# Attention's first head: slabs rounded ahead of the stream's norm, evacuations ahead of the rope, swap ahead of the key pages

## The chip, the cores and the metric

One NeuronCore of a Trainium2 chip runs the whole program. The metric is the device time in microseconds (us) of one launch. Engines: TensorE (PE in the profile; PEld is its weight load), VectorE (DVE), ScalarE (ACT), GpSimd (POOL), and SyncE (SP), which issues all DMAs here.

## The reference

One inference step of a two-layer decoder, width 1024, on a prompt of 1024 tokens and 8 samples of 8 tokens, side by side as T = 1088 columns. Layer 0 is a gated delta rule and a squared-ReLU MLP. Layer 1 is differential attention over 8 heads, each with two maps of 64 channels, and a second MLP. What the change touches is where layer 1 begins:

```python
kv = rmsnorm(h, ln_kv) @ w_kv                       # shared keys and values
k = rope(rmsnorm(kv_k.reshape(..., 8, 2, 64), k_norm), pos)
q = rope(rmsnorm((rmsnorm(h, ln_mix) @ w_q).reshape(..., 8, 2, 64), q_norm), pos)
s = q @ keys.T * 64 ** -0.5                         # keys: cached pages (samples), own keys
p = softmax(where(mask, s, min)); a = p[0] - lam * p[1]
```

The rope turns the first 16 of each map's 64 channels. The samples' cached keys lie in pages that `page_table` names (16 pages of 128 tokens).

## The kernel before

Activations are kept channel-major: `XH` and `XL` hold the stream as a high and a low part (128 x 8 chunks x 1092 columns, in three groups of 364). A product runs over *slabs* of weights, 1024 x 128. A slab is loaded by SyncE into one of two buffers (`load_slab`, L176), scaled by the norm's gain on GpSimd (`scale_slab`, L183), rounded to its high half on ScalarE (`hi_slab`, L189), and its low half is the difference, on VectorE (`lo_slab`, L193). `slab_products` (L203) then does, for each of 8 chunks, three products (high x high, high x low, low x high) by three column groups: 72 matmuls. Slab n's load waits for slab n-2's low half; its rounding waits for slab n-2's products. Semaphores are counters; `Steps.at(i, k)` is the value after step k of round i.

The order of work on each engine is written out by hand. Every engine executes its list in order, so an instruction that waits holds all behind it.

The last part of layer 0's MLP makes the stream's final chunks: a product into PSUM banks 0 to 2 and then one into 3 to 5, each added to `ACC` on VectorE (L1636, `mlp0.free`, numbers 94 and 95 are the last two), then `x_hi` on ScalarE (L1610), `x_lo` on VectorE (L1643, `x_ready`), and the squares summed on GpSimd (L1664).

Then attention's head 0, outside the loop over heads. Its three slabs are k (number 0), q (1) and v (2), in banks 0 to 2, 3 to 5 and 0 to 2:

- TensorE (`att_first_head_tensor`): slab 0's products, the sum of squares over the stream (three matmuls with ones, L2009, `b_sum`), slab 1's products with three `kq_sum` matmuls (L1903) in front of chunks 3, 4 and 5 (they sum the squares of k by map), slab 2's with those of q. Then, in `body`, transposes of the cached keys (L2027), of the new keys (L2043, they need all nine evacuated units, `b_ev.at(0)`, and k's rope), of the values (L2056), and the samples' scores against the cached keys (L2064, they need q's rope).
- ScalarE (`att_scalar`): the stream's norm, three Ln and an Exp into `RSTD` (`b_rs`); slab 1's rounding; squares, Ln and Exp for k; slab 2's rounding; the same for q; the rounding of head 1's k slab, `att_slab(0, 1, 0)`.
- VectorE (`att_vector`): evacuates slab 0 (three `unit_out`, L2407, times `RSTD`), makes ten constants (`constants`, L2393 to L2402, they wait for the constants' DMAs, `b_in`), slab 1's low half, k's norm (`normed`, L2417), slab 2's low half, k's rope in three steps (L2434, L2436, L2439), then evacuates slab 1, and so on; v is evacuated behind q's rope.
- SyncE (`att_sync`): when all of the stream and its sums are made, it loads the tables of the rope and other constants over the MLP's buffers (L1821), the page table (L1822), reads the 16 page numbers into registers (`value_load`, L1825), and goes on with slab 2, 16 pages of cached keys (`key_pages`, L1834), head 1's k slab, the swap of k's rope halves (`swap`, four small DMAs, L1842 and L1843, behind `b_nm`), head 1's q slab, and q's swap.
- GpSimd (`att_gpsimd`) scales slabs 1, 2, head 1's k and q, in this order.

The loop body over heads interleaves head h's attention with head h+1's products by a written order. It isn't changed.

Of the kernel before, what the change touches and what calls it, by code (L numbers as in the profile page):

```python
# [117 lines left out]
def program(nc, x_prompt, x_sample, cache_k, cache_v, page_table, state_delta, state_conv,  # L118
# [1609 lines left out]
    b_in = nc.alloc_semaphore("att_constants_in")  # L1728
# [51 lines left out]
    def att_load(sp, j, a, s):  # L1780
        src = w_q_b[0] if s == 1 else w_kv
        off = a * P + (D if s == 2 else 0)
        load_slab(sp, att_slab(j, a, s), src[:, ds(j * 2 * P + off, P)].rearrange("(k p) c -> p k c", p=P))
# [19 lines left out]


    def att_sync(sp):
        mlp0.x_ready(sp, KC - 1)
        sp.wait_ge(b_sum.sem, b_sum.at(0))
        tables = rope_tables()
        mask = np.zeros((P, 4 * P + NS), np.float32)
        q, k = np.arange(P)[:, None], np.arange(P)[None, :]  # L1810
        for n, full in enumerate((np.eye(P), np.where(k > q, NEG, 0.0))):
            for part in range(2):
                rows = full[part * B_HD:(part + 1) * B_HD]
                mask[:, (2 * n + part) * P:(2 * n + part + 1) * P] = np.concatenate([rows, rows])
        q, k = (np.arange(P) % NS)[:, None], np.arange(NS)[None, :]
        mask[:, 4 * P:] = np.where((q // NQ == k // NQ) & (k % NQ <= q % NQ), 0.0, NEG)
        for dst, a, name in ((COS[:, :], tables[:, 0], "c_cos"), (SIN[:, :], tables[:, 1], "c_sin"),
                             (BO64[:, :], np.kron(np.eye(2), np.ones((B_HD, B_HD))), "c_map_ones"),
                             (STK[:, :], np.concatenate([np.eye(NS)] * 2), "c_stack"),
                             (MASKF[:, :], mask, "c_masks")):  # L1820
            sp.dma_start(dst, nc.inline_tensor(np.ascontiguousarray(a.astype(np.float32)), name).ap()).then_inc(b_in, 16)  # L1821
        sp.dma_start(PGT[:, :], page_table.rearrange("b n -> (b n)").rearrange("(a n) -> a n", a=1)).then_inc(b_in, 16)  # L1822
        sp.wait_ge(b_in, 16 * 6)

        pages = [ds(sp.value_load(PGT[0:1, n:n + 1], min_val=0, max_val=cache_k.shape[0] - 1), 1)  # L1825
                 for n in range(NB * NPG)]

        def key_pages(h, before=None):
            head = ds(h, 1)
            for n in range(NB * NPG):  # L1830
                src = cache_k[pages[n], :, head, :, :].rearrange("a t b m d -> (a t b) (m d)")
                if n == 0 and before is not None:
                    sp.wait_ge(b_pv.sem, b_pv.at(before, SAMPLE_AT + 1))
                sp.dma_start(CP[:, n, :], src).then_inc(b_kin, 16)  # L1834

        def swap(a, i):
            s = i[1]
            i = 2 * i[0] + s
            sp.wait_ge(b_nm.sem, b_nm.at(i))
            for m in range(2):  # L1840
                one, two = (slice(m * B_HD + c * ROT // 2, m * B_HD + (c + 1) * ROT // 2) for c in range(2))
                sp.dma_start(SWP[one, :], KS[a][s][two, 0:T]).then_inc(b_dx, 16)  # L1842
                sp.dma_start(SWP[two, :], KS[a][s][one, 0:T]).then_inc(b_dx, 16)  # L1843

        att_load(sp, 0, 0, 2)
        key_pages(0)
        att_load(sp, 0, 1, 0)
        swap(0, (0, 0))
        att_load(sp, 0, 1, 1)
        swap(0, (0, 1))  # L1850

        def body(j, a):
            h = 2 * j + a
            last = is_head(j, a, H - 1)
            if not last:
                att_load(sp, j, a + 1, 2)
            head, cols_h = ds(h, 1), ds(h * P, P)
            for n in range(NB * NPG):
                src = cache_v[pages[n], :, head, :].rearrange("a t b d -> (a t b) d")
                if n == 0:  # L1860
                    sp.wait_ge(b_pt.sem, b_pt.at(h))
                elif n == NB * NPG - 1:
                    sp.wait_ge(b_kc.sem, b_kc.at(h))
                sp.dma_start(CP[:, n, :], src).then_inc(b_vin, 16)
            sp.dma_start(k_prompt[0].rearrange("t h m d -> t (h m d)")[:, cols_h].rearrange("(u p) c -> p u c", p=P),
                         KTM[:, 0:NT, :]).then_inc(b_ko, 16)
            sp.dma_start(k_sample.rearrange("b q h m d -> (b q) (h m d)")[:, cols_h], KTM[0:NS, NT, :]).then_inc(b_ko, 16)
            sp.wait_ge(b_vc.sem, b_vc.at(h))
            sp.dma_start(v_prompt[0].rearrange("t h d -> t (h d)")[:, cols_h].rearrange("(u p) c -> p u c", p=P),
                         VT[:, 0:NT, :]).then_inc(b_vo, 16)  # L1870
            sp.dma_start(v_sample.rearrange("b q h d -> (b q) (h d)")[:, cols_h], VT[0:NS, NT, :]).then_inc(b_vo, 16)
            if last:
                return
            if is_head(j, a, H - 2):
                proj_b.load(sp, 0, 0)
            else:
                att_load(sp, j, a + 2, 0)
            swap(1 - a, (h + 1, 0))
            key_pages(h + 1, before=h)
            if is_head(j, a, H - 2):  # L1880
                proj_b.load(sp, 0, 1)
            else:
                att_load(sp, j, a + 2, 1)
            swap(1 - a, (h + 1, 1))

        over_heads(sp, body)
# [97 lines left out]
    def att_first_head_tensor(pe):  # L1984
        for s in range(3):
            n = att_slab(0, 0, s)
            pe.wait_ge(w_lo.sem, w_lo.at(n.n))
            if s == 2:
                pe.wait_ge(b_ev.sem, b_ev.at(0, 3))
            for k in range(KC):  # L1990
                if s == 0:
                    mlp0.x_ready(pe, k)
                if s > 0 and 3 <= k < 6:
                    if s == 1 and k == 3:
                        pe.wait_ge(b_ct.sem, b_ct.at(NBC - 1))
                        pe.wait_ge(b_rs.sem, b_rs.at(0, 3))
                    elif s == 2 and k == 3:
                        pe.wait_ge(b_ln.sem, b_ln.at(0, 3))
                    elif k == 5:
                        pe.wait_ge(b_ln.sem, b_ln.at(s - 1, 1))  # L2000
                    kq_sum(pe, 0, s - 1, k - 3, 6 + (k - 3) % 2)
                mm = slab_products(n, 3 * (s % 2), XH, XL, [k], KC)
            mm.then_inc(w_used.sem, 1)
            if s == 0:
                pe.wait_ge(mlp0.sums.sem, mlp0.sums.at(KC - 1))
                for c in range(3):
                    if c == 2:
                        pe.wait_ge(b_rs.sem, b_rs.at(0, 1))
                    nc.tensor.matmul(PS[:, 6 + c % 2, 0:WIDTH[c]], ONES[:, :], SQA[:, c * GRP:c * GRP + WIDTH[c]],  # L2009
                                     start=True, stop=True).then_inc(b_sum.sem, 1)  # L2010

    def att_tensor(pe):
        pe.wait_ge(mlp0.free.sem, mlp0.free.at(95))
        att_first_head_tensor(pe)

        def body(j, a):
# [204 lines left out]

    def att_scalar(act):
        exp_ln_set()
        for c in range(3):
            act.wait_ge(b_sum.sem, b_sum.at(0, c + 1))
            nc.scalar.activation(RSTD[:, c * GRP:c * GRP + WIDTH[c]], PS[:, 6 + c % 2, 0:WIDTH[c]], ACT.Ln,
                                 scale=1.0 / D, bias=EPS).then_inc(b_rs.sem, 1)
# [2 lines left out]
        act.wait_ge(b_rs.sem, b_rs.at(0))  # L2230
        mlp0.x_ready(act, KC - 1)

        hi_slab(act, att_slab(0, 0, 1))
        for s in range(2):
            for g in range(3):
                att_square(act, 0, 0, s, g)
                if g >= 1:
                    att_ln(act, 0, s, g - 1, 6 + (g - 1) % 2)
            att_ln(act, 0, s, 2, 6)
            att_rstd(act, 0, s)  # L2240
            hi_slab(act, att_slab(0, 0, 2) if s == 0 else att_slab(0, 1, 0))

        def body(j, a):
            h = 2 * j + a
# [145 lines left out]
    def att_vector(dve):  # L2390
# [47 lines left out]
                dve.wait_ge(b_rp.sem, b_rp.at(i, 2))  # L2438
                nc.vector.tensor_tensor(t, t, SWP[:, :], ALU.add).then_inc(b_rp.sem, 1)  # L2439

        dve.wait_ge(b_rs.sem, b_rs.at(0))
        for s in range(3):
            dve.wait_ge(w_used.sem, w_used.at(att_slab(0, 0, s).n))
            for g in range(3):
                unit_out(0, s, g, 3 * (s % 2) + g)
            if s == 0:
                constants()
                lo_slab(dve, att_slab(0, 0, 1))
            if s < 2:
                normed(0, 0, s)  # L2450
                lo_slab(dve, att_slab(0, 0, 2) if s == 0 else att_slab(0, 1, 0))
                for step in range(3):
                    rope(0, 0, s, step)

        def body(j, a):
            h = 2 * j + a
# [259 lines left out]
```

## Time and profile before

| | |
|---|---|
| median of 3 runs | 3540.38 us (3538.64 to 3541.57) |
| profiled execution, its time | 3543.65 us |
| its span in the trace | 3541.8 us |
| mean granted TensorE clock | 0.967 |
| TensorE (matmuls) busy | 3308.3 us, 93% |
| VectorE, ScalarE, GpSimd busy | 43%, 32%, 17% |
| mean DMA rate | 45 GB/s |

The page gives averages over the whole program. The stretch that the change touches is some 90 us long, from 1914 to 2003 us; it is read from the timelines of each engine, with a view of windows that shows the TensorE clock which the throttle granted (1.00 is 2.4 GHz, 0.50 is 1.2 GHz). An instruction's idle time stands in brackets, with what ended it.

### The profile page before, as it was taken

How to read it: one execution, taken by the hardware profiler on the slowest of the kernel's cores; microseconds unless marked ns; L12 is line 12 of the kernel's file. 1: busy time of each engine (PE TensorE's matmuls, PEld its weight loads, DVE VectorE, ACT ScalarE, POOL GpSimd, SP SyncE). 2: the span in 40 equal slices, each digit the busy share in tenths (PEclk: the TensorE clock that was granted, in tenths of full speed). 3: DMA queues.
4: the chain of work that ended last, by engine and by line, in shares of the span. 5: the costliest groups of instructions: out<-in, count | busy, mean ns of one | idle time of the engine just before them, and what ended most of it. 6: DMA issues, size and time to landing. Idle time of an engine off the chain costs nothing. (4 is left out here: it accounts for less than half of the span.)

```text
span 3541.8 us, 59935 instructions
## 1 busy us (share of the span) xinstructions
PE 3308.3 (93%) x23951; PEld 3163.5 (89%) x23951; DVE 1521.3 (43%) x2295; ACT 1131.9 (32%) x2096; POOL 613.5 (17%) x421
## 2 busy tenths in 40 slices
PE   5899888988879999999998899999989999999998
PEld 4888878887869999999998788888879999999998
DVE  2555555555537222232224455555557232232222
ACT  3443444344431311111113344444551211111111
POOL 0212221123202311111112100000001311111110
PEclk7999999999969999999999999999999999999999
DMA  2010110011001111111111222222211111111111
GB/s 90 22 32 26 32 33 26 26 32 38 20 26 42 42 45 46 42 48 48 42 45 39 70 59 59 59 62 66 61 38 42 42 47 44 48 43 48 42 45 66
DMA packets 255565, 157.90 MB, mean 45 GB/s; under 512 B 10016, under 2 KB 252082, under 8 KB 255282
## 3 DMA queue, kind: packets, MB, share of 16 engines
q1 hardware_dynamic: 255306, 154.08, 15.1%
q8 instruction: 208, 3.41, 0.4%
q14 instruction: 51, 0.42, 0.0%
HBM read 133.39 MB, written 18.42 MB: 43 GB/s over the span
## 5 line engine op out<-in xcount | busy, mean ns | idle before, releaser
L203 PE MATMUL ps<-x_hi,w_hi 128*128 128x364 f32 (+1 forms) x2304 | 544.9, 344 | 18.5 <-DVE w_lo L193 11.9
L203 PE MATMUL ps<-x_lo,w_hi 128*128 128x364 f32 (+1 forms) x2304 | 510.2, 330 | 0.0
L203 PE MATMUL ps<-x_hi,w_lo 128*128 128x364 f32 (+1 forms) x2304 | 507.9, 329 | 0.0
L193 DVE TENSOR_TENSOR w_lo<-w_raw,w_hi 128x1024 fp32r<-128x1024 f32 x200 | 287.2, 1436 | 469.2 <-ACT w_hi L189 469.1
L189 ACT ACTIVATE w_hi<-w_raw 128x1024 fp32r<-128x1024 f32 x200 | 211.7, 1058 | 809.1 <-PE ps L203 594.2
L183 POOL TENSOR_TENSOR w_raw<-w_raw,params 128x1024 f32<-128x1024 f32 x120 | 237.3, 1977 | 1251.5 <-DMA w_raw<-in_w_in_a 446.3
L203 PEld LDWEIGHTS ps<-x_hi,w_hi 128*128 128x128 f32 x2304 | 396.9, 190 | 46.8 <-DVE w_lo L193 13.6
L203 PEld LDWEIGHTS ps<-x_lo,w_hi 128*128 128x128 f32 x2304 | 401.3, 189 | 0.0
L203 PEld LDWEIGHTS ps<-x_hi,w_lo 128*128 128x128 f32 x2304 | 400.9, 189 | 0.0
L1636 DVE TENSOR_TENSOR acc<-ps,acc 128x1092 f32<-128x1092 f32 x128 | 165.6, 1294 | 435.3 <-PE ps L203 435.3
L203 PE MATMUL ps<-hidden_hi,w_hi 128*128 128x364 f32 (+1 forms) x1536 | 339.2, 329 | 0.0
L203 PE MATMUL ps<-hidden_hi,w_lo 128*128 128x364 f32 (+1 forms) x1536 | 338.4, 328 | 0.0
L203 PE MATMUL ps<-hidden_lo,w_hi 128*128 128x364 f32 (+1 forms) x1536 | 338.3, 328 | 0.0
L1656 POOL TENSOR_TENSOR hidden_lo<-tmp,hidden_hi 128x1092 fp32r<-128x1092 f32 x64 | 162.9, 2545 | 798.7 <-ACT hidden_hi L1605 798.7
L203 PEld LDWEIGHTS ps<-hidden_lo,w_hi 128*128 128x128 f32 x1536 | 266.4, 189 | 0.0
L203 PEld LDWEIGHTS ps<-hidden_hi,w_hi 128*128 128x128 f32 x1536 | 266.2, 188 | 0.0
L203 PEld LDWEIGHTS ps<-hidden_hi,w_lo 128*128 128x128 f32 x1536 | 266.1, 188 | 0.0
L1603 ACT ACTIVATE tmp<-tmp 128x1092 f32<-128x1092 f32 x64 | 71.5, 1118 | 416.6 <-DVE tmp L1625 416.6
L1625 DVE SCALAR_TENSOR_TENSOR tmp<-ps,rstd 128x1092 f32<-128x1092 f32 x64 | 82.9, 1296 | 243.7 <-PE ps L203 235.5
L1896 PE MATMUL ps<-x_hi,w_hi 128*128 128x364 f32 (+1 forms) x504 | 175.9, 349 | 4.1 <-DVE mix L2407 3.9
L1896 PE MATMUL ps<-x_hi,w_lo 128*128 128x364 f32 (+1 forms) x504 | 165.2, 328 | 0.0
L1896 PE MATMUL ps<-x_lo,w_hi 128*128 128x364 f32 (+1 forms) x504 | 165.0, 327 | 0.0
(365 smaller groups left out, 5153.7 us busy)
## 6 DMA issues: line engine op xcount, KB each, us to landing
w_raw<-in_w_up SPq DMA_DIRECT2D x64, 512.0 KB, 3.9
w_raw<-in_w_down SPq DMA_DIRECT2D x64, 512.0 KB, 3.4
w_raw<-in_w_in_a SPq DMA_DIRECT2D x32, 512.0 KB, 4.2
w_raw<-in_w_kv SPq DMA_DIRECT2D x16, 512.0 KB, 3.8
cache_pages<-in_cache_k SPq DMA_DIRECT2D x128, 64.0 KB, 1.9
cache_pages<-in_cache_v SPq DMA_DIRECT2D x128, 64.0 KB, 1.9
x_in<-in_x_prompt SPq DMA_DIRECT2D x8, 512.0 KB, 4.4
state_sample<-in_state_delta SPq DMA_DIRECT2D x8, 512.0 KB, 4.0
```

The source lines that it names most:

```text
L183: nc.gpsimd.tensor_tensor(RAW[s.slot][:, :, :], RAW[s.slot][:, :, :], gain(g).unsqueeze(2).to_broadcast([P, KC, P]), ALU.mult).then_inc(w_ ...
L189: nc.scalar.activation(WH[s.slot][:, :, :], RAW[s.slot][:, :, :], ACT.Copy).then_inc(w_hi.sem, 1)
L193: nc.vector.tensor_tensor(WL[s.slot][:, :, :], RAW[s.slot][:, :, :], WH[s.slot][:, :, :].bitcast(F32), ALU.subtract).then_inc(w_lo.sem, 1)
L203: mm = nc.tensor.matmul(PS[:, bank + g, 0:WIDTH[g]], wt, x[:, k, g * GRP:g * GRP + WIDTH[g]], start=(k == 0 and t == 0), stop=(k == chunks ...
L1603: nc.scalar.activation(t, t, ACT.Square).then_inc(self.hid.sem, 1)
L1625: nc.vector.scalar_tensor_tensor(grouped(TMP[up][:, :]), banks(3 * op), 0.0, grouped(RSTD[:, :]), ALU.max, ALU.mult).then_inc(self.free.se ...
L1636: nc.vector.tensor_tensor(grouped(ACC[:, m, :]), banks(3 * ((op + a) % 2)), grouped(ACC[:, m, :]), ALU.add).then_inc(self.free.sem, 1)
L1656: nc.gpsimd.tensor_tensor(HID[par][1][:, s, :], TMP[up][:, :], HID[par][0][:, s, :].bitcast(F32), ALU.subtract).then_inc(self.lo.sem, 1)
L1896: mm = nc.tensor.matmul(PS[:, bank, 0:WIDTH[g]], w[s.slot][:, k, :], x[:, k, g * GRP:g * GRP + WIDTH[g]], start=(k == 0 and t == 0), stop= ...
```

## The change

Nothing is computed otherwise. In the stretch at head 0:

- SyncE issues slab 2's load first, in front of its waits for the stream and the sums; k's swap is issued in front of the 16 key pages, and head 1's two slab loads then follow the pages back to back.
- TensorE starts slab 0 when evacuation 94 is done (banks 0 to 2), and waits for 95 in front of slab 1. The `kq_sum`s move from chunks 3 to 5 to chunks 4 to 6. The wait for the made constants moves from slab 1 to slab 2; slab 1 waits instead for the constants' DMAs (`b_in`), in front of its first `kq_sum`.
- ScalarE rounds slab 1 in front of the stream's norm, and slab 2 right behind it, in front of k's squares.
- VectorE makes slab 1's low half first, evacuates slab 0, makes slab 2's low half, the constants, k's norm; then it evacuates slab 1 in front of k's rope; then q's norm, the low half of head 1's k slab, the evacuation of slab 2 (v), and q's rope last.

```diff
@@ att_sync @@
+        att_load(sp, 0, 0, 2)
         mlp0.x_ready(sp, KC - 1)
         sp.wait_ge(b_sum.sem, b_sum.at(0))
...
-        att_load(sp, 0, 0, 2)
+        swap(0, (0, 0))
         key_pages(0)
         att_load(sp, 0, 1, 0)
-        swap(0, (0, 0))
         att_load(sp, 0, 1, 1)
         swap(0, (0, 1))
@@ att_first_head_tensor @@
             pe.wait_ge(w_lo.sem, w_lo.at(n.n))
+            if s == 1:
+                pe.wait_ge(mlp0.free.sem, mlp0.free.at(95))
             if s == 2:
                 pe.wait_ge(b_ev.sem, b_ev.at(0, 3))
...
-                if s > 0 and 3 <= k < 6:
-                    if s == 1 and k == 3:
+                if s > 0 and 4 <= k < 7:
+                    if s == 1 and k == 4:
+                        pe.wait_ge(b_in, 16 * 6)
+                        pe.wait_ge(b_rs.sem, b_rs.at(0, 3))
+                    elif s == 2 and k == 4:
                         pe.wait_ge(b_ct.sem, b_ct.at(NBC - 1))
-                        pe.wait_ge(b_rs.sem, b_rs.at(0, 3))
-                    elif s == 2 and k == 3:
                         pe.wait_ge(b_ln.sem, b_ln.at(0, 3))
-                    elif k == 5:
+                    elif k == 6:
                         pe.wait_ge(b_ln.sem, b_ln.at(s - 1, 1))
-                    kq_sum(pe, 0, s - 1, k - 3, 6 + (k - 3) % 2)
+                    kq_sum(pe, 0, s - 1, k - 4, 6 + k % 2)
@@ att_tensor @@
-        pe.wait_ge(mlp0.free.sem, mlp0.free.at(95))
+        pe.wait_ge(mlp0.free.sem, mlp0.free.at(94))
@@ att_scalar @@
         exp_ln_set()
+        hi_slab(act, att_slab(0, 0, 1))
         for c in range(3):
...
-        hi_slab(act, att_slab(0, 0, 1))
+        hi_slab(act, att_slab(0, 0, 2))
         for s in range(2):
...
-            hi_slab(act, att_slab(0, 0, 2) if s == 0 else att_slab(0, 1, 0))
+            if s == 1:
+                hi_slab(act, att_slab(0, 1, 0))
@@ att_vector @@
-        dve.wait_ge(b_rs.sem, b_rs.at(0))
-        for s in range(3):
+        def first_units(s):
             dve.wait_ge(w_used.sem, w_used.at(att_slab(0, 0, s).n))
             for g in range(3):
                 unit_out(0, s, g, 3 * (s % 2) + g)
-            if s == 0:
-                constants()
-                lo_slab(dve, att_slab(0, 0, 1))
-            if s < 2:
-                normed(0, 0, s)
-                lo_slab(dve, att_slab(0, 0, 2) if s == 0 else att_slab(0, 1, 0))
-                for step in range(3):
-                    rope(0, 0, s, step)
+        lo_slab(dve, att_slab(0, 0, 1))
+        dve.wait_ge(b_rs.sem, b_rs.at(0))
+        first_units(0)
+        lo_slab(dve, att_slab(0, 0, 2))
+        constants()
+        normed(0, 0, 0)
+        first_units(1)
+        for step in range(3):
+            rope(0, 0, 0, step)
+        normed(0, 0, 1)
+        lo_slab(dve, att_slab(0, 1, 0))
+        first_units(2)
+        for step in range(3):
+            rope(0, 0, 1, step)
```

## Rows read from the trace of the kernel before

**Rows 1.** The page: busy time of TensorE, its share, its instructions.

```profile
PE 3308.3 (93%) x23951; PEld 3163.5 (89%) x23951; DVE 1521.3 (43%) x2295; ACT 1131.9 (32%) x2096; POOL 613.5 (17%) x421
```

**Rows 2.** TensorE's timeline: start, duration, line, operation, in brackets idle before and releaser.

```profile
1918.28 0.77 PE L203 MATMUL ps<-x_hi,w_hi 128*128 128x364 f32 x3 [3.40 <-DVE acc L1636]
...
1931.86 2.21 PE L2009 MATMUL ps<-sq_sum,ones 128*128 128x364 f32 x6
1944.94 1.28 PE L203 MATMUL ps<-x_hi,w_hi 128*128 128x364 f32 x3 [10.87 <-DVE w_lo L193]
...
1954.04 0.77 PE L1903 MATMUL ps<-kq_squared,map_ones 128*128 128x364 f32 x2
...
1956.14 0.77 PE L1903 MATMUL ps<-kq_squared,map_ones 128*128 128x364 f32 x2
...
1971.20 1.55 PE L1903 MATMUL ps<-kq_squared,map_ones 128*128 128x364 f32 x2 [5.30 <-ACT kq_squared L2188]
...
1992.11 2.15 PE L2043 MATMUL ps<-ident,k_even 128*128 128x128 f32 x9 [9.09 <-DVE mix L2407]
...
1997.68 3.82 PE L2064 MATMUL ps<-cache_keys_t,q_by_batch 128*128 128x256 f32 x16
```

**Rows 3.** Windows: stretch, length, busy time by engine (instructions), TensorE clock, DMA.

```profile
1919.60:1922.90 3.30, 3.30 (x13) 3.30 (x12) 1.11 (x1) 2.23 (x2) 2.22 (x1) 0.50 0.00 0
...
1992.10:1997.70 5.60, 5.59 (x27) 5.52 (x28) 0.36 (x3) 3.62 (x8) 0.00 (x0) 0.50 0.06 17
```

**Rows 4.** VectorE's timeline, end of the MLP to head 0.

```profile
1913.26 1.29 DVE L1636 TENSOR_TENSOR acc<-ps,acc 128x1092 f32<-128x1092 f32 x1
...
1919.41 1.30 DVE L1643 TENSOR_TENSOR x_lo<-acc,x_hi 128x1092 fp32r<-128x1092 f32 x1 [1.18 <-ACT x_hi L1610]
...
1958.61 1.35 DVE L2417 SCALAR_TENSOR_TENSOR k_even<-k_even,params,kq_rstd 128x1092 f32<-128x1092 f32 x1 [13.73 <-ACT kq_rstd L2201]
...
1964.67 1.29 DVE L2434 TENSOR_TENSOR kq_swapped<-kq_swapped,rope_sin 128x1088 f32<-128x1088 f32 x1 [3.57 <-DMA kq_swapped<-k_even]
...
1987.76 2.87 DVE L2439 TENSOR_TENSOR q_even<-q_even,kq_swapped 128x1088 f32<-128x1088 f32 x1
1990.55 1.41 DVE L2407 TENSOR_TENSOR mix<-ps,rstd 128x364 f32<-128x364 f32 x3
```

**Rows 5.** SyncE, page numbers into registers: durations ns min/median/max, first and last start.

```profile
L1825 SPq TENSOR_LOAD <-page_numbers x16: 263/267/493, 1940.3 to 1948.8; - x16
```

**Rows 6.** SyncE's timeline: DMA issues.

```profile
1949.36 0.40 SPq L176 DMA_DIRECT2D w_raw<-in_w_kv  x1
1949.95 8.16 SPq L1834 DMA_DIRECT2D cache_pages<-in_cache_k  x16
1958.15 0.43 SPq L176 DMA_DIRECT2D w_raw<-in_w_kv  x1
1959.99 0.81 SPq L1842 DMA_DIRECT2D kq_swapped<-k_even  x1
...
1962.89 0.44 SPq L176 DMA_DIRECT2D w_raw<-in_w_q_b  x1
```

**Rows 7.** Slab tiles, 1880 to 2010: durations ns min/median/max, first and last start.

```profile
L189 ACT ACTIVATE w_hi<-w_raw x7: 1040/1059/1062, 1882.6 to 2007.4; 128x1024 fp32r<-128x1024 f32 x7
L193 DVE TENSOR_TENSOR w_lo<-w_raw,w_hi x7: 1218/1226/2564, 1883.7 to 2009.3; 128x1024 fp32r<-128x1024 f32 x7
```

**Rows 8.** GpSimd's timeline, same stretch.

```profile
1923.16 1.90 POOL L183 TENSOR_TENSOR w_raw<-w_raw,params 128x1024 f32<-128x1024 f32 x1
...
1962.24 1.90 POOL L183 TENSOR_TENSOR w_raw<-w_raw,params 128x1024 f32<-128x1024 f32 x1 [7.08 <-DMA w_raw<-in_w_kv]
...
1987.36 2.12 POOL L183 TENSOR_TENSOR w_raw<-w_raw,params 128x1024 f32<-128x1024 f32 x1 [18.44 <-DMA w_raw<-in_w_kv]
```

**Rows 9.** Start of the program: SyncE's slab loads and GpSimd's first scale.

```profile
40.37 45.97 SPq L176 DMA_DIRECT2D w_raw<-in_w_in_a  x4
...
45.24 1.90 POOL L183 TENSOR_TENSOR w_raw<-w_raw,params 128x1024 f32<-128x1024 f32 x1 [44.78 <-DMA w_raw<-in_w_in_a]
```

## The prediction

> **What bounds the kernel now.** Page first: TensorE is busy 93% of the span [rows 1], so time comes out only where TensorE stands still or runs slowly. Its timeline, read from the end of layer 0's MLP to the first scores of head 0, has four holes [rows 2]: 3.40 us in front of slab 0 (k), 10.87 in front of slab 1 (q), 5.30 inside slab 2 (v, in front of the first key-norm sum), 9.09 in front of the key transposes. The granted clock (windows) is the second thing to see: it falls to half (1.2 GHz) behind them, 0.50 in 1919.6 to 1922.9 and in 1992.1 to 1997.7 [rows 3]. Matmuls there take twice the time: the 3.3 us stretch costs 1.65. From the last hole on, TensorE works nearly without a pause, so what moves the start of the key transposes (1992.11) or of the cached-score products (1997.68) moves the end as much.
>
> Next what ends each hole. Hole 1 is the last MLP evacuation (DVE, bank group 3 to 5). Hole 2 is a DVE queue: norm, evacuation of slab 0, the constants' arrival, ten constants, and only then slab 1's low half. Hole 3: slab 1's evacuation stands behind the k rope, which waits for the swap. Hole 4 is the v evacuation, which stands behind the q rope: 1990.55, key transposes at 1992.11, 1.56 later [rows 2, 4]. SyncE is the last view: the page numbers' register loads run from 1940.3 to 1948.8 [rows 5], its next issue is at 1949.36, 16 key pages take 8.2, then come a slab load, the swap and another slab load [rows 6].
>
> **The change, step by step.** No instruction is added but waits; everything is order. I lay the new order out on the old clock, taking durations and lags from the rows.
>
> *Slab 0.* TensorE now waits for evacuation 94 (ends 1914.55), not 95. Its last MLP matmul ends at 1914.88 (1918.28 less 3.40), so with the usual overlap slab 0 starts at about 1914.75. The chunk waits don't bite: the last x_lo is ready at 1920.71 and chunk 7 is needed at about 1925.2. Slab 0 took 13.58 (1918.28 to 1931.86); without the half-clock stretch it is 13.58 - 1.65 = 11.93, or 1.49 a chunk. The norm's sums start at 1926.7 and not 1931.86: everything keyed to them moves **5.2 us** earlier [rows 2 to 4].
>
> *Slab 1 rounded early.* POOL's scale ends at 1925.06, ScalarE rounds until 1926.17 (in front of the first Ln, which can't start before the sums do, at 1926.7), VectorE subtracts. The early load of slab 2 lets POOL run its scale at the same moment (1925.06 to 1927.0), and a two-input VectorE operation beside POOL ends about 1.1 after it: the k and q rope adds took 2.87 instead of 1.29 so, and slab subtractions go from 1.22 up to 2.56 [rows 4, 7, 8]. So w_lo is there at 1928.1, and TensorE wants it at about 1928.7 (three sums of 0.61, which is 2.10 - 1.49 of the rows below, and a short wait for the first Ln). Cost nothing, cover 0.6; if it is gone, TensorE waits some tenths, hidden by what follows.
>
> *Slab 1 and 2 products.* The constants arrive 5.2 earlier too, 1940.3 - 5.2 = 1935.1, and the sum in front of chunk 4 (1928.7 + 4 x 1.49 = 1934.7) waits 0.4. A sum and its chunk take 2.10 (1954.04 to 1956.14) [rows 2, 5]. Slab 1 then ends at 1935.1 + 3 x 2.10 + 1.49 = 1942.9. Slab 2 needs slab 0's evacuation (it stands in front of the constants on VectorE, so before 1935.1), the q squares (slab 1's evacuation from 1943.1, 1.41 for three units, squares behind it unit by unit, the first needed at 1948.9) and the constants (they were done before w_lo of slab 1, so now before 1944.94 - 5.2 = 1939.7): no wait. It ends at 1942.9 + 5 x 1.49 + 3 x 2.10 = 1956.7. Holes 1 to 3 are gone, with their slow stretches.
>
> *SyncE's queue is what then binds.* The register loads still start when the constants are there and take 9.06 (1940.3 to 1949.36): SyncE is free at 1944.2. The k norm is ready before that: third sum of slab 1 at 1939.3, plus 2.47 (1956.14 to 1958.61) and 1.35, is 1943.1. So the swap, now in front of the pages, goes out at 1944.2 and takes 2.9 (1959.99 to 1962.89); its data are there 4.7 after issue (1959.99 to 1964.67), at 1948.9, and the k rope is done at 1952.7, long before it is needed. The key pages take 8.2 (1949.95 to 1958.15): until 1955.3. Behind them is the load of head 1's k slab. From its issue to POOL's scale it took 4.09 (1958.15 to 1962.24) with nothing large behind it [rows 2, 4, 6, 8].
>
> *The new tail.* The diff puts this slab's subtraction in front of the v evacuation, and key transposes need that. The chain: issue 1955.3, landing 4.09, scale 1.90, round 1.06, subtract 1.23, handovers 0.1: 1963.7; then 1.56 to the transposes: 1965.3. Two additions. First, head 1's q slab is issued right behind (no swap between them) and its scale follows at 1961.3 to 1963.3; by the rule of the rows the subtraction ends at 1964.4, so +0.7. Second, two loads at once: at the program's start two went out together (the first at 40.37) and the first one's scale began at 45.24, 4.87 later; so up to +0.8, and 0 at least; I take +0.3, nearer to the 4.09 of this stage [rows 7 to 9]. Key transposes at **1966.3**, against 1992.11: 25.8 earlier. TensorE is then idle from about 1958.3 (slab 2's end, and two groups of cached-key transposes after the last page lands) to 1966.3, some 8 us instead of 9.09, and starts at half clock as before: no difference there.
>
> *The q rope.* Its norm is ready near 1957.0, its swap near 1961.7, but it stands behind the v evacuation: multiplications from 1966.1 (the evacuation takes 1.41), last add 1968.6 to 1969.9, four copies 0.6, 1970.5. The products that need it came 5.57 behind the first key transpose (1992.11 to 1997.68): 1971.9. Covered by 1.4. But head 1's v slab, loaded when w_lo is free (1964.7), has its scale near 1968.7; if it catches the add, as in both ropes of the trace, that ends at 1971.8 and the products wait 0.5. I take half: 0.3 [rows 2, 4, 8].
>
> **Sum.** 25.8 - 0.3 = 25.5 us. Checked by terms: moved sums 5.2; old stretch from the sums to the key transposes 60.25 (1931.86 to 1992.11), new one 39.6 (1926.7 to 1966.3), 20.65; less 0.3: 25.5. Of the holes and slow stretches, slabs 1 and 2 give up more than that, but some 8 us reappear as one wait. Profiled execution: 3543.65 - 25.5 = 3518.2; before, it lies 3.3 over the median of the runs, so on the median: 3540.4 - 25.5 = **3514.9 us**. What a measurement here can tell from no change is 0.2%, 7.1 us.
>
> A rule to weigh at the two loads: the Trainium skill, "DMA: Bandwidth & Descriptors", section "Queues, rings and completion order", says that on each DMA engine descriptors are consumed in ring order, which for two loads of one issuing engine speaks for +0 instead of my +0.3. By it the sum would be 25.8. The start's 4.87 speaks against it, unless it comes of something else there; no row tells.
>
> A rule that speaks against the change: the Trainium skill, "GPSIMD Engine Reference", section "Key points", has VectorE instructions with two SBUF inputs contend with GpSimd. The trace agrees (2.87 against 1.29). Were each of the new order's VectorE two-input operations near a scale caught for the full 1.9, the sum would be about 23.
>
> **Rivals.**
> 1. *The tail chain is longer than drawn* (0.22). Slab load, page issues, or collisions with POOL. The load at 4.87 is 0.5 more than drawn, a certain collision of the rope add 0.3 more, one or two further collisions of 1.6 (2.87 - 1.29) or pages that SyncE issues a tenth slower 1 to 5: gain 20 to 24, 3516 to 3521. For it: all of it is serial on SyncE, POOL, ScalarE and VectorE, with no cover. Against: every link has a row.
> 2. *A new pause on TensorE puts the clock down* (0.08): without holes TensorE runs 42 us in a row; a hole of 3 us in it costs 3 and 1.65 of clock. In slabs 1 and 2 that hides behind the 8 us wait; only in slab 0 or in head 0 behind does it cost 4.7: gain 20 to 21, 3519 to 3520.
> 3. *A longer gain* (0.1): the slab 2 end (1956.7) would be the gate if the load were early. It isn't, so the bound is the links at their best: no collision, +0 for both: 26.5, and 1 to 2 more if the half clock after the wait ends sooner than after 1992.1: 3512 to 3514.
> 4. *Not faster* (0.05, of it slower 0.03): one mechanism. The v evacuation now hangs on head 1's k slab, which nothing at this place needs yet. If that slab's w_lo came 25 us later than drawn, at 1990, the gain is gone, and behind that it is slower by as much. Price: every us of load or scale, 1 for 1. Against: the largest time from load issue to scale that I rest on is 4.87, and the slab's buffer is free long before, at the subtraction of slab 1.
>
> Forecast 0.55 (24.5 to 26.5: 3513.9 to 3515.9). For 8 in 10 I take rival 3 and most of 1 and 2: 3511 to 3521. Faster 0.95, within 0.2% 0.02, slower 0.03.
>
> **What would show it.** After: slab 0 follows the MLP without a hole, clock 1.0 through it; sums 5.2 earlier; no hole in front of slab 1, at most 0.5 us at its chunk 4; none in slab 2; one hole of 7 to 9 us in front of the key transposes, ended by the v evacuation; in front of that VectorE idles for w_hi of head 1's k slab, ScalarE for POOL, POOL for the load, SyncE for nothing. The page register loads end before the swap is issued, within a microsecond of it. From the first scores on, both traces agree but for the shift. Wrong would be: a stall in head 0's loop body that takes part of the shift back, a load of more than 5 us, or w_lo of slab 1 later than the sums.

## The result, and the profile after

The changed kernel takes 3508.9 us (median of 4 runs, 3508.1 to 3510.9) against 3539.5 for the one before (4 runs, 3537.2 to 3541.6). The ratio is 0.9918, with a 95% interval of 0.9904 to 0.9932, so the gain is 29 us, 24 to 34 (the two medians lie 30.6 apart). Forecast were 25.5 us and 3514.9, with a range of 3511 to 3521: faster was right, the time lies 2.1 us below the range.

The two profiled executions have spans of 3541.8 and 3506.3 us, 35.5 apart, more than the medians. To keep the stage apart from the rest, times in it are given from the end of TensorE's last MLP matmul: 1914.88 before, 1913.61 after.

TensorE's timeline after, from slab 0 to the first product of the loop over heads (start, duration, line, operation, in brackets idle time and releaser); it answers to [rows 2]:

```profile
1913.44 0.66 PE L203 MATMUL ps<-x_hi,w_hi 128*128 128x364 f32 x3
...
1925.36 2.21 PE L2012 MATMUL ps<-sq_sum,ones 128*128 128x364 f32 x6
1927.13 0.94 PE L203 MATMUL ps<-x_hi,w_hi 128*128 128x364 f32 x3
...
1933.83 0.88 PE L1903 MATMUL ps<-kq_squared,map_ones 128*128 128x364 f32 x2 [0.30 <-DMA page_numbers<-in_page_table]
...
1951.91 0.77 PE L1903 MATMUL ps<-kq_squared,map_ones 128*128 128x364 f32 x2
...
1955.83 1.09 PE L2030 MATMUL ps<-ident,cache_pages 128*128 128x128 f32 x8 [0.18 <-DMA cache_pages<-in_cache_k]
...
1964.53 2.15 PE L2046 MATMUL ps<-ident,k_even 128*128 128x128 f32 x9 [7.60 <-DVE mix L2412]
...
1970.38 3.72 PE L2067 MATMUL ps<-cache_keys_t,q_by_batch 128*128 128x256 f32 x16 [0.28 <-DVE q_by_batch L2477]
...
1975.37 0.44 PE L1896 MATMUL ps<-x_hi,w_hi 128*128 128x364 f32 x1
```

Slab 0 follows the MLP without a hole, the sums come at +11.75 (before +16.98), slab 1 follows them at once, 0.30 us are waited for the constants, and slab 2 has no hole. One hole of 7.60 is left in front of the key transposes, which start at +50.92 (before +77.23). The first product of the loop comes at +61.8, before at +87.9: 26.1 us.

The same stretch as windows (stretch, length, busy time by engine with instructions, granted TensorE clock, DMA share, GB/s), to compare with [rows 3]:

```profile
1913.60:1925.30 11.70, 11.70 (x73) 11.70 (x72) 4.10 (x4) 6.41 (x6) 8.46 (x4) 1.00 0.14 41
1925.30:1955.60 30.30, 30.00 (x164) 27.06 (x162) 14.70 (x23) 11.21 (x19) 0.42 (x1) 1.00 0.30 91
1956.80:1964.50 7.70, 0.13 (x2) 0.01 (x1) 3.27 (x5) 2.03 (x3) 3.75 (x2) 0.68 0.42 125
1964.50:1970.30 5.80, 5.57 (x26) 5.29 (x26) 5.72 (x7) 3.80 (x9) 3.00 (x1) 0.55 0.36 104
1970.30:1975.40 5.10, 5.02 (x40) 4.42 (x40) 1.02 (x6) 0.73 (x3) 0.00 (x0) 1.00 0.46 130
```

The clock stays at its upper level (1.00, 2.4 GHz) for 42 us of products and for the cached-score products. It is low only over the one hole (0.68) and for the transposes behind it (0.55).

What ends that hole is read on the other engines. SyncE's issues after, for [rows 6]:

```profile
1942.81 0.80 SPq L1843 DMA_DIRECT2D kq_swapped<-k_even  x1
...
1945.86 8.36 SPq L1835 DMA_DIRECT2D cache_pages<-in_cache_k  x16
1954.27 0.43 SPq L176 DMA_DIRECT2D w_raw<-in_w_kv  x1
1954.75 0.58 SPq L176 DMA_DIRECT2D w_raw<-in_w_q_b  x1
1955.76 0.97 SPq L1843 DMA_DIRECT2D kq_swapped<-q_even  x1
```

GpSimd (the first and second line are two scales each, back to back), for [rows 8]:

```profile
1921.97 3.75 POOL L183 TENSOR_TENSOR w_raw<-w_raw,params 128x1024 f32<-128x1024 f32 x2
1958.22 3.75 POOL L183 TENSOR_TENSOR w_raw<-w_raw,params 128x1024 f32<-128x1024 f32 x2 [32.49 <-DMA w_raw<-in_w_kv]
1966.86 3.00 POOL L183 TENSOR_TENSOR w_raw<-w_raw,params 128x1024 f32<-128x1024 f32 x1 [4.90 <-DMA w_raw<-in_w_kv]
```

VectorE (L2422 is a norm, L2412 the evacuations, L2444 the last step of a rope, L2476 the first copy for the cached scores), for [rows 4]:

```profile
1925.00 1.81 DVE L193 TENSOR_TENSOR w_lo<-w_raw,w_hi 128x1024 fp32r<-128x1024 f32 x1 [5.56 <-ACT w_hi L189]
...
1940.68 1.35 DVE L2422 SCALAR_TENSOR_TENSOR k_even<-k_even,params,kq_rstd 128x1092 f32<-128x1092 f32 x1 [3.51 <-issue]
...
1949.96 1.29 DVE L2444 TENSOR_TENSOR k_even<-k_even,kq_swapped 128x1088 f32<-128x1088 f32 x1
1954.38 1.36 DVE L2422 SCALAR_TENSOR_TENSOR q_even<-q_even,params,kq_rstd 128x1092 f32<-128x1092 f32 x1 [3.12 <-ACT kq_rstd L2204]
1961.23 1.81 DVE L193 TENSOR_TENSOR w_lo<-w_raw,w_hi 128x1024 fp32r<-128x1024 f32 x1 [5.50 <-ACT w_hi L189]
1962.97 1.41 DVE L2412 TENSOR_TENSOR mix<-ps,rstd 128x364 f32<-128x364 f32 x3
...
1966.81 1.29 DVE L2444 TENSOR_TENSOR q_even<-q_even,kq_swapped 128x1088 f32<-128x1088 f32 x1
1968.14 1.77 DVE L2476 COPY q_all_batches<-q_even 64x64 f32<-64x64 f32 x1
```

VectorE stands idle 5.50 us for head 1's k slab to be rounded, though slab 2's products end near 1955.7; POOL waits for the load, the load for the pages, the pages for the swap. The v evacuation starts at 1962.97, the key transposes 1.56 later, as before.

### The profile page after: what moved, and what is told of

Same layout as the page of the kernel before. It is cut to its first block and busy times, and to the rows that moved or that the text cites. A ratio compares the mean times of both kernels' runs of the same rounds, so it can differ in the third digit from the quotient of the medians.

```text
span 3506.3 us, 59936 instructions
## 1 busy us (share of the span) xinstructions
PE 3292.3 (94%) x23951; PEld 3147.2 (90%) x23951; DVE 1518.9 (43%) x2295; ACT 1131.2 (32%) x2096; POOL 611.6 (17%) x421
```

## The experiments

The rows "kernel before" and "changed kernel" are the four runs each of the result. Every other kernel was timed later, in five rounds beside the kernel before, and its ratio is to the runs of those rounds. The three columns on the right are read from each kernel's trace, in us from the end of the MLP. "First product" is the start of TensorE's first product of the loop over heads.

| run | median us | ratio to before (95%) | key transposes | cached scores | first product |
|---|---|---|---|---|---|
| kernel before | 3539.5 | | +77.2 | +82.8 | +87.9 |
| again_before | 3537.7 | 1.0003 (0.9990 to 1.0016) | +78.8 | +83.7 | +88.6 |
| round1_only | 3539.3 | 1.0012 (0.9999 to 1.0025) | +77.8 | +82.7 | +87.6 |
| slab0_only | 3531.3 | 0.9987 (0.9977 to 0.9997) | +72.2 | +77.1 | +82.0 |
| changed kernel | 3508.9 | 0.9918 (0.9904 to 0.9932) | +50.9 | +56.8 | +61.8 |
| again_after | 3508.9 | 0.9932 (0.9920 to 0.9944) | +51.2 | +57.0 | +62.0 |
| rope_first | 3517.5 | 0.9943 (0.9926 to 0.9959) | +52.0 | +60.0 | +67.8 |
| swap_behind | 3518.1 | 0.9945 (0.9926 to 0.9964) | +53.7 | +61.7 | +68.4 |
| pages_early | 3509.5 | 0.9919 (0.9905 to 0.9934) | +50.1 | +56.1 | +61.1 |
| v_first | 3508.8 | 0.9920 (0.9905 to 0.9935) | +43.7 | +53.8 | +60.7 |
| best | 3508.0 | 0.9917 (0.9901 to 0.9932) | +43.9 | +53.0 | +61.0 |
| sums_early | 3507.2 | 0.9910 (0.9895 to 0.9925) | +43.8 | +51.1 | +58.5 |
| best_warm | 3504.7 | 0.9903 (0.9887 to 0.9919) | +43.9 | +53.0 | +58.0 |
| filled | 3498.4 | 0.9888 (0.9869 to 0.9907) | +43.8 | +50.0 | +54.9 |

### Where the gain outside the stage comes from: both kernels again

> The kernel before, unchanged, profiled a second time and timed against itself. The stretch from TensorE's first to its last product of the loop over heads took 582.1 us in the first profile before and 576.0 after, though its code is the same. Theory 1 (half-clock stretches in the loop fall differently in every execution): this profile's stretch lies anywhere in 575 to 584, its TensorE clock by head between 0.94 and 1.00 in another pattern than the first. Theory 2 (the change itself speeds the loop up by some 5 us): it is 581 to 583 again. Time 3539 to 3541, ratio 1.000.

> The changed kernel, unchanged, profiled a second time. Theory 1: the loop's stretch is anywhere in 573 to 584, so that the two kernels' stretches overlap; the local gain up to head 0's first product is again 26 us counted from the end of the MLP. Theory 2: it is 575 to 577 again. Both: time 3508 to 3515, ratio 0.991 to 0.993.

The loop over heads, from its first to its last product, in the kernel before, the changed kernel, and the kernel before profiled again (TensorE's products of one line: durations ns min/median/max, first and last start):

```profile
L1896 PE MATMUL ps<-x_hi,w_hi x504: 322/327/606, 2002.8 to 2584.9; 128*128 128x364 f32 x126, 128*128 128x360 f32 x42
```

```profile
L1896 PE MATMUL ps<-x_hi,w_hi x504: 322/327/606, 1975.4 to 2551.1; 128*128 128x364 f32 x126, 128*128 128x360 f32 x42
```

```profile
L1896 PE MATMUL ps<-x_hi,w_hi x504: 321/328/606, 2002.8 to 2580.5; 128*128 128x364 f32 x126, 128*128 128x360 f32 x42
```

582.1, 575.7 and 577.7 us, and 577.5 in the changed kernel's second profile. Theory 1 holds: the first pair's 6.4 us are one execution's scatter, not the change. All the other kernels have the same loop too: 574.7 to 579.6. The windows of heads 0 to 3 in the changed kernel (from one head's cached-score products to the next head's) show what can scatter:

```profile
1970.38:2052.69 82.31, 80.21 (x567) 72.78 (x568) 48.27 (x101) 40.35 (x108) 5.75 (x3) 1.00 0.24 65
2052.69:2137.58 84.89, 83.07 (x570) 74.51 (x568) 49.04 (x102) 40.86 (x111) 5.70 (x3) 0.96 0.23 60
2137.58:2218.32 80.74, 79.69 (x570) 72.57 (x568) 46.16 (x102) 41.14 (x111) 6.68 (x3) 1.00 0.24 65
2218.32:2306.74 88.42, 85.34 (x569) 75.81 (x568) 49.33 (x102) 40.80 (x110) 5.75 (x3) 0.94 0.22 59
```

The same number of matmuls takes 80.7 or 88.4 us, and the granted clock is 1.00 or 0.94.

The times of the kernel before scatter as well. Over the 77 runs that all these comparisons hold it has a mean of 3537.4 us (3524.6 to 3549.7, standard deviation 5.2); the changed kernel has 3509.5 over 10 runs (3508.1 to 3512.1, 1.4). The difference of the means is 28.0 (3537.43 less 3509.48).

Of that the stage holds 26.4: the two profiles of the kernel before have the first product at +87.90 and +88.62, those of the changed kernel at +61.76 and +62.03. The other 1.6 lie outside it. The stretch from the loop's last product to the end of the program takes 956.3 to 956.9 us in the four profiles with the old order (slab0_only and round1_only among them) and 954.8 to 956.4 in the ten with the new one, on average 1.0 less. No run was made to find out why.

### Parts alone

```diff
@@ att_first_head_tensor, in before: slab0_only @@
+            if s == 1:
+                pe.wait_ge(mlp0.free.sem, mlp0.free.at(95))
@@ att_tensor @@
-        pe.wait_ge(mlp0.free.sem, mlp0.free.at(95))
+        pe.wait_ge(mlp0.free.sem, mlp0.free.at(94))
```

> The kernel before with only the wait in front of slab 0 relaxed (evacuation 94, and 95 in front of slab 1). Theory A (everything behind hangs on the norm's sums, through SyncE and VectorE): the hole of 3.4 us and the half clock behind it go, 1.7, the sums start 13.5 - 1.6 = 11.9 us after slab 0, and all behind moves 5.2 earlier: 3535, ratio 0.9985. Rival (another chain, anchored elsewhere, ends the later holes, which then grow): the key transposes stay where they were against the MLP's end, ratio 1.000.

The sums moved from +16.98 to +11.75, the first product by 5.9 to 6.6 against the two profiles of before. The time fell by 5.9 by the medians and 4.6 (1 to 8) by the ratio. The other three holes kept their lengths (10.83, 5.51, 9.08), so theory A is right: everything behind hangs on the sums.

```diff
@@ att_scalar, in before: round1_only @@
         exp_ln_set()
+        hi_slab(act, att_slab(0, 0, 1))
...
-        hi_slab(act, att_slab(0, 0, 1))
@@ att_vector @@
+        lo_slab(dve, att_slab(0, 0, 1))
         dve.wait_ge(b_rs.sem, b_rs.at(0))
...
                 constants()
-                lo_slab(dve, att_slab(0, 0, 1))
```

> The kernel before with only slab 1's rounding (ScalarE) and its low half (VectorE) in front of the norm; loads, swap and evacuations as before. Theory A (SyncE's serial queue binds): slab 1 starts right behind the sums, but its first sum waits at chunk 3 for the constants until about 1943.7, and slab 2's load, the pages and the swap still go out at 1949.4 to 1962.9, so the holes move but the key transposes come only 1 to 2 us earlier: gain 1 to 4 with what the clock gives, 3536 to 3539. Rival (the 10.87 us hole is worth what it shows): gain 10.9 to 13.4, 3526 to 3529.

TensorE's waits in it up to slab 2:

```profile
1939.24 1.58 PE L1903 MATMUL ps<-kq_squared,map_ones 128*128 128x364 f32 x2 [5.19 <-DVE softmax_scalars L2402]
...
1954.06 0.76 PE L203 MATMUL ps<-x_hi,w_hi 128*128 128x364 f32 x3 [2.81 <-DVE w_lo L193]
```

The hole of 10.87 has broken in two, 5.19 for the constants and 2.81 for slab 2's weights, and 5.71 and 9.08 follow as before. The key transposes are at +77.8 (before +77.2 and +78.8), and the time isn't shorter: theory A, without the gain of 1 to 4 that it allowed. The longest hole of [rows 2] was worth nothing by itself: behind it stood SyncE's queue and VectorE's rope.

### Parts taken back

```diff
@@ att_vector, in the changed kernel: rope_first @@
-        first_units(1)
         for step in range(3):
             rope(0, 0, 0, step)
+        first_units(1)
```

> The changed kernel with k's rope in front of slab 1's evacuation on VectorE, as before the change. The rope waits for the swap's data (1947.4) and ends at 1951.2 on the changed kernel's clock, so slab 1 is evacuated at 1951.2 to 1952.6 and not at 1942.0 to 1943.4. Theory A: q's squares then reach TensorE at 1952.7 instead of 1947.7, a hole of 5 us opens in slab 2 with half clock behind it, q's norm ends 5 to 6 later, q's rope ends at 1971 to 1973 and the cached-score products start 2 to 4 later than 1970.4: 3512 to 3514. Rival (the last hole's 7.6 us absorb it): no change, 3509.

The hole opened, TensorE's first q sum:

```profile
1950.80 1.55 PE L1903 MATMUL ps<-kq_squared,map_ones 128*128 128x364 f32 x2 [4.54 <-ACT kq_squared L2191]
```

So the rival is out. The hole cost more than theory A had it, 5.9 us at the first product and 8.6 in the median: the cached-score products came 3.1 later, and then ran 6.54 us instead of 3.72, at a granted clock of 0.56.

```diff
@@ att_sync, in the changed kernel: swap_behind @@
-        swap(0, (0, 0))
         key_pages(0)
         att_load(sp, 0, 1, 0)
+        swap(0, (0, 0))
```

> The changed kernel with k's swap issued behind the key pages and head 1's k slab, as before the change. The pages go out at 1942.7 to 1951, the slab load at 1951.1, 3.2 us earlier, the swap at 1951.6 to 1954.4. Theory A (the last hole hangs on the slab load behind the pages): key transposes would come 3 earlier, but k's rope now ends at about 1960.2 and q's norm, its swap and rope follow: q's swap out near 1961.5, landed 1966.2, rope done 1970: about the time of the changed kernel, 0 to 2 us slower. Rival (moving the swap was worth much): the k rope's delay of 10 us goes through to the end, 6 to 10 us slower, 3515 to 3519.

The rival was right (3518.1, the first product 6.5 later). VectorE in this run (k's rope, then q's norm):

```profile
1953.65 1.80 DVE L2439 TENSOR_TENSOR kq_swapped<-kq_swapped,rope_sin 128x1088 f32<-128x1088 f32 x1 [13.48 <-DMA kq_swapped<-k_even]
1955.37 1.28 DVE L2441 TENSOR_TENSOR k_even<-k_even,rope_cos 128x1088 f32<-128x1088 f32 x1
1956.68 2.87 DVE L2444 TENSOR_TENSOR k_even<-k_even,kq_swapped 128x1088 f32<-128x1088 f32 x1
1960.08 1.36 DVE L2422 SCALAR_TENSOR_TENSOR q_even<-q_even,params,kq_rstd 128x1092 f32<-128x1092 f32 x1 [0.53 <-DVE k_even L2444]
```

K's rope waits 13.48 for its data and then stands twice behind a scale of POOL's (1.80 and 2.87 instead of 1.29); q's norm stands behind it on VectorE, and behind that q's own swap and rope. The rope that my prediction called "done long before it is needed" has a margin of only a few us: in the changed kernel it ends at 1951.25 and q's norm starts at 1954.38.

These two runs and slab0_only price three moves of the change, at 5.9, 6.5 and some 6 us of the first product's start. They need not add up. The other 8 or so of the 26 were not tested move by move: the early rounding of slabs 1 and 2, the early load of slab 2, v's evacuation ahead of q's rope, and the sums one chunk later.

```diff
@@ att_sync, in the changed kernel: pages_early @@
         att_load(sp, 0, 0, 2)
+        sp.dma_start(PGT[:, :], page_table...).then_inc(b_in, 16)
+        sp.wait_ge(b_in, 16)
+        pages = [ds(sp.value_load(PGT[0:1, n:n + 1], ...), 1) for n in range(NB * NPG)]
         mlp0.x_ready(sp, KC - 1)
...
-        sp.dma_start(PGT[:, :], page_table...).then_inc(b_in, 16)
-        sp.wait_ge(b_in, 16 * 6)
-        pages = [ds(sp.value_load(PGT[0:1, n:n + 1], ...), 1) for n in range(NB * NPG)]
```

> The changed kernel with the page table loaded and its 16 numbers read into registers while TensorE still does slab 0 (9 us taken off SyncE's queue behind the constants). Theory A as predicted (SyncE's queue binds, but only down to k's norm, which ends at 1942.0 against the swap's issue at 1942.8): gain 0.8 and nothing more, 3508. Rival (the register loads are worth their 9 us): 3500.

0.8 to 1.1 us at the key transposes and 0.6 to 0.9 at the first product, as expected; the time can't tell it from nothing. The 9 us of register loads had only been covering k's norm: it now ends at 1941.06, and the swap goes out at 1941.10.

### The last hole

```diff
@@ att_vector, in the changed kernel: v_first @@
-        lo_slab(dve, att_slab(0, 1, 0))
         first_units(2)
         for step in range(3):
             rope(0, 0, 1, step)
+        lo_slab(dve, att_slab(0, 1, 0))
```

> The changed kernel with the v evacuation and q's rope in front of the low half of head 1's k slab on VectorE. Theory A (that slab's load, scale, rounding and low half end the last hole): the hole of 7.6 us in front of the key transposes goes, but the cached-score products wait for q's rope, whose swap lands at about 1960.4, so they start near 1965.5 and not 1970.4: gain 4 to 6 against the changed kernel, about 3504; more if the clock stays up. Rival (the last key page or ScalarE's rounding, which stands in front of the cached keys' copies, ends it): gain under 2, 3507 to 3509.

TensorE (key transposes, second half of the cached keys, cached-score products):

```profile
1956.98 1.17 PE L2046 MATMUL ps<-ident,k_even 128*128 128x128 f32 x9 [0.48 <-DVE mix L2412]
1961.44 1.97 PE L2030 MATMUL ps<-ident,cache_pages 128*128 128x128 f32 x8 [3.29 <-ACT cache_keys_t L2256]
...
1967.04 5.62 PE L2067 MATMUL ps<-cache_keys_t,q_by_batch 128*128 128x256 f32 x16 [1.71 <-DVE q_by_batch L2477]
```

The hole in front of the key transposes is gone and they are 7.2 us earlier, so what stood there was head 1's k slab. But the wait came back as 3.29 for ScalarE, which waits for that slab's scale and rounds it before it copies the cached keys, and as 1.71 for q's rope; and the cached-score products took 5.62 instead of 3.72. Left of 7.2 are 1.1 to 1.3, and the median (3508.8) is that of the changed kernel. Theory A had the cause right and the gain of 4 to 6 wrong.

```diff
@@ att_sync, in pages_early: best @@
-        swap(0, (0, 0))
         key_pages(0)
         att_load(sp, 0, 1, 0)
+        swap(0, (0, 0))
         att_load(sp, 0, 1, 1)
@@ att_scalar @@
-            if s == 1:
-                hi_slab(act, att_slab(0, 1, 0))
...
                 if g >= 1:
                     att_ln(act, 0, s, g - 1, 6 + (g - 1) % 2)
+                elif s == 1:
+                    hi_slab(act, att_slab(0, 1, 0))
@@ att_vector @@
+        lo_slab(dve, att_slab(0, 1, 0))
         normed(0, 0, 1)
-        lo_slab(dve, att_slab(0, 1, 0))
```

> The changed kernel with the page numbers read early, the key pages and head 1's k slab in front of k's swap, and that slab rounded behind q's first square and subtracted in front of q's norm. Theory A: nothing of the last hole's chain is left, v is evacuated when slab 2 ends; key transposes near 1957.3 instead of 1964.5, the cached-score products behind q's rope at about 1965: gain 5 to 6, or more with the clock: 3502 to 3504. Rival (as for v_first: something else stands there): gain under 2.

```profile
1957.96 1.17 PE L2046 MATMUL ps<-ident,k_even 128*128 128x128 f32 x9 [0.74 <-DVE mix L2412]
...
1967.09 6.77 PE L2067 MATMUL ps<-cache_keys_t,q_by_batch 128*128 128x256 f32 x16 [5.65 <-DVE q_by_batch L2477]
```

The rival's number came (a gain under 2), but not its reason: the key transposes came 7 us earlier and ran at full clock (1.17 instead of 2.15), and it is the products that wait 5.65 for q's rope and then take 6.77. What remains is 0.7 to 1.0. To test whether the hole itself makes them slow:

```diff
@@ body, in best: best_warm @@
+            if first:
+                for x in range(26):
+                    nc.tensor.matmul(PS[:, 6, 0:GRP], WH[0][:, x % KC, :], XH[:, x % KC, 0:GRP],
+                                     start=True, stop=True)
             pe.wait_ge(b_qz.sem, b_qz.at(h))
```

> The kernel of run best, with 26 products of slab 2's weights and the stream's first group (4.3 us of TensorE work into an unused bank, results thrown away) in its last hole, in front of the cached-score products. In best that hole was 5.65 us and the 16 products behind it took 6.77 us instead of 3.72, at half clock. Theory C (an idle hole sets the clock to half for what comes behind it, and there it costs 3): the hole shrinks to 1.3, the products take 3.7, the first product of the loop comes 3 us earlier; 3504 to 3505. Rival (the products are slow for another reason, traffic or operands): they take 6.8 again.

```profile
1959.51 4.54 PE L2066 MATMUL ps<-x_hi,w_hi 128*128 128x364 f32 x26
1965.41 3.72 PE L2071 MATMUL ps<-cache_keys_t,q_by_batch 128*128 128x256 f32 x16 [1.35 <-DVE q_by_batch L2481]
```

The products start at the same +53.0 and take 3.72: 3.0 us won by work that is thrown away. The granted clock over them is 1.00, and 0.54 in best. DMA traffic, the rival, isn't equal (113 against 202 GB/s), but it isn't needed: in twelve traces these 16 products took 3.61 to 6.77 us at clocks from 1.00 to 0.54, and time times clock is 3.6 to 3.7 each time. So a hole's length is one part of its price, and what stands behind it at half clock is the other. The program's times agree (3508.0 and 3504.7), but their intervals overlap; what shows it is the stage.

```diff
@@ att_first_head_tensor, in best: sums_early @@
-                if s > 0 and 4 <= k < 7:
+                if s > 0 and 6 - 2 * s <= k < 9 - 2 * s:
...
-                    kq_sum(pe, 0, s - 1, k - 4, 6 + k % 2)
+                    kq_sum(pe, 0, s - 1, k - 6 + 2 * s, 6 + k % 2)
```

Head 1's k slab is rounded and subtracted behind q's norm again.

> The kernel of run best with the sums of q's squares in front of chunks 2 to 4 of slab 2 instead of 4 to 6, and head 1's k slab rounded and subtracted behind q's norm again. Theory D (the last hole now hangs on q's rope, which hangs on the third q sum): q's norm 3 us earlier and right behind k's rope, swap out at +39 us from the MLP's end, landed at +43.7, rope done +47.6, products at +48.5 to +49.5 instead of +53.0; the hole in front of them is under 2 us and the clock stays up: first product of the loop at +54 instead of +61, 3501 to 3503. Rival (the cached keys' copies on ScalarE or the v transposes end it): gain under 2.

Half of it: the products at +51.1 instead of +49 (k's rope add stood behind POOL's scale of head 1's q slab, 2.87 instead of 1.29, and q's norm behind that; q's own last add stood behind the next scale, 2.87 again). A hole of 3.86 was left, and behind it the clock was 0.60 and the products took 6.15 us. The first product is at +58.5, not +54, and the median 3507.2. The last run takes both lessons:

```diff
@@ att_sync, in sums_early: filled @@
+        att_load(sp, 0, 1, 1)
         swap(0, (0, 0))
-        att_load(sp, 0, 1, 1)
         swap(0, (0, 1))
```

The discarded products are those of best_warm, with `range(18)`.

> The kernel of run sums_early with two things more: 18 products with discarded results (3.0 us) in front of the cached-score products, as in best_warm, and head 1's q slab loaded in front of k's swap, so that its scale doesn't meet k's rope add (2.87 us there instead of 1.29). Theory C and D together: q's rope 1.6 us earlier, cached-score products at +49.5 us from the MLP's end instead of +51.1, and 3.7 us long instead of 6.15: first product of the loop at +54.5 (sums_early +58.6, best_warm +58.0, changed kernel +61.9), 3501 to 3503. Rival: what is won goes into the hole, +57 to +58, 3505.

No wait over 0.8 us is left between the MLP and the loop over heads (3.2 us of it are the discarded products); the first product is at +54.9 (expected +54.5), 7.0 earlier than in the changed kernel. The time is 3498.4 us, some 10 below the changed kernel and 40 below the kernel before; that is 3 to 5 less than expected, of which the stage explains nothing.

## Why the prediction was off

**Right, step by step.** Slab 0 without a hole and the sums 5.2 earlier (+11.8 drawn, +11.75 measured; slab0_only shows that all behind follows). Slab 1's low half, beside POOL's scale, drawn at +13.2 and measured at 1926.81, +13.2 (its duration 1.81 shows the contention). The wait at chunk 4: 0.4 drawn, 0.30. The swap's issue behind the register loads: +29.3 drawn, +29.2. Head 1's k slab issued at +40.4 drawn, +40.7. The last hole, 8 us drawn, 7.60, with the v evacuation as its end and head 1's k slab as its cause (v_first). The wait for q's copies, 0.3 drawn and 0.28 measured (0.46 in again_after), is right by luck: the rope's last add began 0.05 us ahead of POOL's scale and took its usual 1.29, the scale was held up to 3.00, and the first copy was held behind the scale (1.77 us). Of the two loads at once: the first scale began 3.95 after the issue (1954.27 to 1958.22), against 4.09 before without a second load behind it, so my +0.3 was wrong. The Trainium skill has each DMA engine consume its descriptors in ring order ("DMA: Bandwidth & Descriptors", section "Queues, rings and completion order"); the trace agrees, with 3.95.

**The size.** For the stage 25.5 us were drawn. The two profiles of each kernel give 88.3 and 61.9 for the first product, 26.4: 0.9 more, of which 0.4 is the load.

**What failed** is the step from the stage to the program: "From the first scores on, both traces agree but for the shift", and with it the base and the width of the range. The stage's number was laid on 3540.38, a median of three runs, and the range was made of the stage's costs alone. Over 77 runs the kernel before has a mean of 3537.4: that is 2.9 us of the 6.0 that the forecast is off. 0.9 is the stage. 1.6 lie in the rest of the program (the means of both kernels differ by 28.0 and the stage explains 26.4), and 3508.9 is 0.6 below the changed kernel's mean. That the 1.6 are real was not shown; with 10 runs on one side and the loop alone scattering over 574.7 to 582.1 in the profiles it need not be. The profiled run, 3.3 above the median of its kernel, had been a sign that single executions scatter by more than the three runs did. Both ratios' intervals (0.9904 to 0.9932, 0.9920 to 0.9944) hold 25.5 us, which is 0.9928.

**The rivals.** The longer tail chain did not come, and the new pause did not either. SyncE did take 11.5 us from the swap's issue to the slab load's, 0.4 more than drawn (the pages 8.36 instead of 8.2), but from that load to the key transposes it was 10.3 and not 11.0. Of the collisions that the prediction prices, the two slab subtractions came about as drawn (1.81 each). The longer gain was nearest, but for another reason than given: the half clock behind the last hole lasted as before. (Its 26.5 is also 0.3 short by its own terms: without any collision the 0.3 for q's copies goes too, 26.8.) The mechanism of the fourth, the v evacuation hanging on head 1's k slab, is what the hole of 7.60 consists of; with a load of 3.95 it was far from its point.

## What to carry to other kernels

Price a hole by the queue that stands behind it, not by its length: 10.87 us were worth nothing alone (round1_only), while the whole reordering of the chain behind it (one norm's sums, SyncE's queue, two ropes) was worth 26. When a hole closes, look at what comes behind the next one: TensorE at half clock took 3 us more for the same 16 products, and throwaway matmuls in the hole gave them back. And lay a blind forecast on a base whose own scatter is known: three runs that agreed within 3 us were still 3 us from the mean of 77.

## What the runs showed that was not expected

- The scatter differs from kernel to kernel. The one before went over 25 us in 77 runs (3524.6 to 3549.7), the changed kernel over 4 in 10 (3508.1 to 3512.1), swap_behind over 22 in 7 (3504.8 to 3526.8). All have the same loop over heads. Why was not settled.
- When a VectorE operation with two inputs in SBUF meets a slab scale on POOL, the one that starts second is held. The prediction's rule ("ends about 1.1 after it") is one half of that. In the stretch around head 0 (1895 to 2012 us), in all 14 traces, an operation that started while a scale ran ended 1.07 to 1.16 us behind the scale's end; where it started first, it took its usual 1.28 to 1.35, and the scale ended 1.75 to 1.80 behind it (up to 3.00 long instead of 1.90). Who starts first can hang on 0.05 us. The same add takes 1.29 in best and 2.87 in best_warm.
- The 64 x 64 copy on VectorE, held behind a scale, took 1.77 us instead of the 0.17 to 0.19 of its like: a small operation waits as long as a large one. The evacuations from PSUM that ran beside a scale were not held (1.42 us for three, as elsewhere).
- The lower clock came behind holes of 3.40 us in the kernel before (1.65 us lost on products), 3.86 in sums_early (2.4) and 2.81 in round1_only (0.59 over the next 4 us); behind the 1.35 us that best_warm left it did not.
